# Neighbourhood attention: bias tiles loaded ready-made by DMA, gate spreads ahead of value products, first q/k pair loaded during the GLA stage, norm sums behind the first slots' turns

## The reference, cut to what matters

```python
def neighbourhood_attention(q, k, v, k_ctx, v_ctx, rpb, rows):
    # q,k,v [B,H,S,d]; window of 8 rows x 16 columns round each token, plus all context keys
    win_rows = jnp.clip(r_idx - kh // 2, 0, rows - kh)[:, None] + jnp.arange(kh)
    win_cols = jnp.clip(c_idx - NA_KW // 2, 0, GRID_W - NA_KW)[:, None] + jnp.arange(NA_KW)
    dcol = win_cols - c_idx[:, None] + (NA_KW - 1)
    def one_row(r):
        drow = rws - r + (NA_KH - 1)
        bias = rpb[:, drow[None, :, None], dcol[:, None, :]]
        s_loc = einsum(qr, kw) * scale + bias
        s_ctx = einsum(qr, k_ctx) * scale
        p = softmax(concatenate([s_loc, s_ctx]))
        return p_loc @ vw + p_ctx @ v_ctx

def combine(o, na, z):           # o: GLA output, na: NA output, z: gate input
    g = head_rmsnorm(merge_heads(o), gla_norm, GLA_HEADS)
    return (concatenate([g, merge_heads(na)]) * silu(z)) @ w_out
```

## Time and profile before

| | us |
|---|---|
| median of 3 runs | 3959.82 (3958.52 to 3967.68) |
| the profiled execution, whole | 3962.81 |
| its span | 3959.9 |
| PE busy in the span | 3876.0 (98%) |
| DVE / ACT / POOL busy | 1831.3 / 973.5 / 935.2 |
| mean granted clock, share of full | 0.991 |

### The profile page before, as it was taken

One profiled execution on the slowest core, in us unless ns is written; L12 is line 12 of the kernel. 1 busy time (PEld: TensorE's weight loads), 2 busy tenths in 40 slices (PEclk: granted clock), 3 DMA queues, 4 the chain that ended last, 5 costly groups with the idle time before them and its releaser, 6 DMA issues. The chain is left out here.

```text
span 3959.9 us, 48043 instructions
## 1 busy us (share of the span) xinstructions
PE 3876.0 (98%) x18138; PEld 2409.1 (61%) x18138; DVE 1831.3 (46%) x3905; ACT 973.5 (25%) x1837; POOL 935.2 (24%) x992
## 2 busy tenths in 40 slices
PE   8999999999999999999999999999999999999998
PEld 4688997786558568567544565656544444444447
DVE  3227884676243366556476222222556442313134
ACT  4224332333124311155225211111122000000000
POOL 0005774001111111134132112113132122222223
PEclk9999999999999999999999999999999999999999
DMA  5420003111211122141131112123243211111113
GB/s 196 152 90 11 8 9 68 42 48 54 85 67 39 51 67 65 59 150 40 48 109 55 53 41 67 45 71 106 81 146 127 75 33 47 48 43 43 43 48 101
DMA packets 113715, 270.22 MB, mean 68 GB/s; under 512 B 15623, under 2 KB 45177, under 8 KB 112398
## 3 DMA queue, kind: packets, MB, share of 16 engines
q1 hardware_dynamic: 106512, 251.81, 19.3%
q0 software_dynamic: 5920, 13.25, 1.4%
q10 hardware_dynamic: 1056, 2.10, 0.2%
HBM read 218.53 MB, written 50.87 MB: 68 GB/s over the span
## 5 line engine op out<-in xcount | busy, mean ns | idle before, releaser
L452 PE MATMUL upper_banks<-sbuf 128*128 128x512 f32 (+1 forms) x2016 | 771.4, 545 | 1.5 <-issue 1.1
L3358 PE MATMUL upper_banks<-sbuf 128*128 128x512 f32 x1400 | 617.1, 596 | 5.0 <-ACT sbuf L3635 3.5
L452 PEld LDWEIGHTS upper_banks<-sbuf 128*128 128x128 f32 x2016 | 382.4, 190 | 388.7 <-issue 374.7
L3358 PEld LDWEIGHTS upper_banks<-sbuf 128*128 128x128 f32 x1400 | 263.3, 191 | 317.9 <-issue 308.2
L2502 PE MATMUL gla_prod<-sbuf 128*128 128x512 f32 x560 | 247.6, 593 | 0.3 <-DVE sbuf L2534 0.3
L608 DVE TENSOR_TENSOR sbuf<-upper_banks,sbuf 128x512 f32<-128x512 f32 (+1 forms) x140 | 81.9, 585 | 283.2 <-PE upper_banks L452 282.6
L404 POOL TENSOR_TENSOR sbuf<-sbuf 128x512 f32<-128x512 f32 x36 | 47.4, 1316 | 655.0 <-DMA sbuf<-in_w_mlp_out 306.9
L1039 PE MATMUL mla_banks<-sbuf 128*128 128x128 f32 x1344 | 175.9, 278 | 5.6 <-POOL sbuf L878 4.4
L2502 PEld LDWEIGHTS gla_prod<-sbuf 128*128 128x128 f32 x560 | 103.6, 190 | 119.9 <-issue 117.4
L1662 PE MATMUL mls_banks<-sbuf 128*128 128x512 f32 x392 | 175.1, 593 | 0.3 <-DVE sbuf L2079 0.3
L1039 PEld LDWEIGHTS mla_banks<-sbuf 128*128 128x128 f32 x1344 | 162.9, 192 | 10.5 <-POOL sbuf L878 7.3
(11 more groups left out here) (564 smaller groups left out, 6599.1 us busy)
## 6 DMA issues: line engine op xcount, KB each, us to landing
sbuf<-in_l_w_in SPq DMA_DIRECT2D x59, 512.0 KB, 4.0
sbuf<-in_w_in SPq DMA_DIRECT2D x52, 512.0 KB, 4.5
sbuf<-in_w_mlp_out SPq DMA_DIRECT2D x40, 512.0 KB, 3.6
sbuf<-in_w_mlp_in SPq DMA_DIRECT2D x32, 512.0 KB, 3.7
sbuf<-in_l_w_mod SPq DMA_DIRECT2D x24, 512.0 KB, 6.2
scratch_gates<-sbuf SPq DMA_DIRECT2D x48, 256.0 KB, 2.0
sbuf<-in_l_w_mod SPq DMA_DIRECT2D x8, 1024.0 KB, 16.6
sbuf<-in_l_w_out SPq DMA_DIRECT2D x16, 512.0 KB, 3.7
```

The lines of the kernel that those rows point to most:

```text
L452: last = nc.tensor.matmul(bank_of(n, c)[:, 0:wd], lw[:, k * P:(k + 1) * P], right_operand(c, base, tw, k, o, wd, to), start=k == 0 and c i ...
L3358: last = nc.tensor.matmul(pb, lw[:, k * P:(k + 1) * P], rhs, start=k == 0 and c in ("P1", "P2", "P5"), stop=k == 3, skip_group_check=True)
```

## The change

- **Bias by DMA.** A new input `na_bias` of 64 x 8192 holds every 64 x 64 bias tile ready. SP loads each half of each `mids` and `edge` tile (64 partitions, 2 KB each) directly, 4 transfers a tile, 20 tiles. One-hot matrices, `table_part`, `table_evict` and POOL's copies go. The factor 8 of the table goes too: q is scaled by 1/8 in the GLA stage instead, in the evictions that exist already.
- **First pair during GLA.** q and k of pair 0 are loaded by SP in the GLA stage after the first z store, to where `na_block` expects them; buffers of the GLA stage move for it. Scores of slot 0 wait for that transfer only. v has its own semaphore.
- **Norm sums.** `gla_sums(0)` and `(1)` follow the scores of slot 0, `(2)` and `(3)` follow the first turns of slots 0 and 1. The four products into the unread bank go. DVE copies the sums to SBUF (32 columns), since their bank is used by slot 1.
- **ACT.** Only `zn[0]` gets its Silu ahead of the slots. The Silu of four `zg` tiles stands after `soft(2)`, that of `zn[1]` to `zn[3]` and the root after `soft(5)`.
- **Spreads ahead.** In slots 8 to 23 the two spreads of the norm factors stand before the value products.
- `zg` lies in `U`, where the table was, so pair 1 no longer waits for POOL's gates.

The diff, cut to its core:

```diff
@@ gla_layer, SP
+                if n == first_z:
+                    for e in range(NE):
+                        sp.wait_ge(stored[e], ...)
+                    sp.dma_start(first_keys[:, 0:NLAT], nq_dram[0:P, :]).then_inc(first_in, 16)
+                    sp.dma_start(first_keys[:, NLAT:], nk_dram[0:P, :]).then_inc(first_in, 16)
@@ na_block, SP
-            for r in range(2):
-                sp.dma_start(lhs[64 * r:64 * r + 33, :], io["rpb"]).then_inc(hot_in, 16)
-                sp.dma_start(hot[r], io["rpb_hot"][:, 4096 * r:4096 * (r + 1)]).then_inc(hot_in, 16)
+            def load_bias(dst, h, e, rr, landed):
+                s0, r0 = NA_FIRST[e]
+                a, d0 = na_rows(s0, r0 + rr)
+                o = NCTX + 64 * a
+                sp.dma_start(dst[64 * rr:64 * rr + 64, o:o + 512], io["na_bias"][:, (16 * h + d0) * 64:(16 * h + d0 + 8) * 64]).then_inc(landed, 16)
+            sp.dma_start(zn[:, 0, :], z_dram[4 * P:5 * P, NCTX:T]).then_inc(zn_first, 16)
+            sp.wait_ge(cleared, 1)
+            middle(0)
+            border(0)
+            load_values(0)
+            border(1)
+            sp.wait_ge(cleared, 2)
+            middle(1)
             sp.dma_start(gl[:], io["l1_gla_norm"]).then_inc(gl_in, 16)
-            load_pair(0)
             for j in range(4):
+                sp.dma_start(zg[j], z_dram[j * P:(j + 1) * P, NCTX:T]).then_inc(zg_in, 16)
+            for j in range(1, 4):
                 sp.dma_start(zn[:, j, :], z_dram[(4 + j) * P:(5 + j) * P, NCTX:T]).then_inc(zn_in, 16)
+            load_keys(1)
+            load_values(1)
...
+            for e in range(2, len(edges)):
+                p = 2 + (e - 6) // 4
+                lead = e in (6, 10)
+                if lead:
+                    middle(p)
+                border(e)
+                if lead:
+                    sp.wait_ge(pv, NU * (p - 1))
+                    load_keys(p)
+                    load_values(p)
+                    if p == 2:
+                        sp.dma_start(H[:, :, NCTX:T], h_dram...).then_inc(h_back, 16)
@@ na_block, PE
-            gla_sums(0)
-            gla_sums(1)
-            for x in range(4):
-                nc.tensor.matmul(banks[:, 5, :], ident[:], osum[:, x, 0:512], start=True, stop=True)
-            pe.wait_ge(hot_in, 64)
-            for b in range(8):
-                table_part(b)
             for i in range(-2, NS + 1):
                 if i + 2 < NS:
                     scores(i + 2)
+                if i == -2:
+                    gla_sums(0)
+                    gla_sums(1)
                 if 0 <= i < NS:
                     turn(i, range(2, nb[i]))
-                if i == -2:
-                    gla_sums(2)
-                    gla_sums(3)
                 if i >= 1:
                     weigh(i - 1)
                 if 0 <= i + 1 < NS:
                     turn(i + 1, range(2))
+                if i in (-1, 0):
+                    gla_sums(3 + i)
@@ na_block, ACT
+            act.wait_ge(zn_first, 16)
+            nc.scalar.activation(zn[:, 0, :], zn[:, 0, :], ACT.Silu).then_inc(zn_up, 1)
             soft(0)
             for i in range(NS):
                 copy(i)
                 if i + 1 < NS:
                     soft(i + 1)
+                if i == 1:
+                    act.wait_ge(zg_in, 64)
+                    for j in range(4):
+                        last = nc.scalar.activation(zg[j], zg[j], ACT.Silu)
+                    last.then_inc(zsil, 1)
+                if i == 4:
+                    act.wait_ge(zn_in, 48)
+                    for j in range(1, 4):
+                        last = nc.scalar.activation(zn[:, j, :], zn[:, j, :], ACT.Silu)
+                    last.then_inc(zn_up, 1)
+                    act.wait_ge(gcopied, 1)
+                    nc.scalar.activation(gcol[:], gcol[:], ACT.Sqrt, bias=eps, scale=1.0 / P).then_inc(grooted, 1)
@@ na_block, DVE
-            for b in range(8):
-                table_evict(b)
+            dve.wait_ge(cleared, 3)
...
+                if i == 0:
+                    dve.wait_ge(osum1, 4)
+                    nc.vector.tensor_copy(gcol[:], banks[:, 7, 256:288]).then_inc(gcopied, 1)
```

249 lines of the change are left out of this document (97 added, 152 removed).

## The result

| | before | after |
|---|---|---|
| median, us | 3960.83 (3958.52 to 3967.68, 4 runs) | 3938.65 (3936.03 to 3940.51, 4 runs) |
| the profiled execution, whole / span | 3962.81 / 3959.9 | 3938.22 / 3936.0 |
| mean granted clock, share of full | 0.991 | 0.992 |

The ratio of the two is 0.994, with a 95% interval of 0.9928 to 0.9952. The changed kernel is 22.2 us faster; the forecast was 15.8 (3959.82 to 3944). The direction and the place were right, and the size was 6.4 us short. The lower end of the stated range, 3938.5, stood for 21.3 us gained on 3959.82; the measured gain is beyond that. Measured once more later (changed_again), the same pair of kernels is 16.3 us apart, with the same gain inside the NA stage.

The account below looks back on a forecast made before the run. PE, busy in 98% of the span, was taken to bound the kernel. 19.4 us gained by slot 3, less 3.7 for ACT's insertions, the rest 0, gave 15.7: from 3959.82 to 3944 us, range 3938.5 to 3952.5.

Parts of the forecast that it names:

- The low start: Start of NA: PE enters about 1677.2 at clock 0.50; scores of slot 0 take 3.35 us, sums 0 and 1 6.51.
- The choice of 1703: Start of the scores of slot 3, taken between 1700.7 and 1705.0; 19.4 us gained against 1722.4.
- the forecast's early case: Head of NA: clock rises during scores of slot 1; scores of slot 3 at 1699.7, about 1700.7 with DVE's work.
- The first tile: First bias tile lands at 1682.6 to 1684.6, `biased` at 1685.5 to 1687.5; PE waits 0 to 0.5 us.
- ACT's insertions: Silus and root behind soft(2) and soft(5) cost PE 1.35 and 2.4 us, together 3.7, range 2.5 to 5.
- Later bias tiles are issued two border slots ahead: SP's queue: tiles issued about 20 us ahead arrive in time despite 4 MB of h between; cost 0.
- Spreads at nothing: Slots 8 to 23: spreads ahead of value products mean same products and same waits, so 0 us.
- 1: Clock stays low through the first slots; two low slots cost 8 us, 7.7 gained, 3952 us; chance 0.17.
- 2: ACT's insertions not covered: 13.5 us lost, 3954 us, or 3951 with the page's drain; chance 0.10 for both.
- 3: Narrow bias transfers are slow, ACT waits for `zg`; at 50 GB/s 27.5 us lost, 3972 us; chance 0.04.
- 5: Another wait holds the first slots where the table did; 0 to 3 us gained, 3958 us; chance 0.05.
- 4: Early clock rise and full cover: slot 3 at 1700.7, 2 us lost to ACT, 3940 us; chance 0.14.

Follow-up runs that it names:

- changed_again: The changed kernel itself, unedited, measured again with the third set of runs; 3944.65 us, ratio 0.9941 to 0.9967 against the kernel before.
- late_start: Changed kernel, but PE's first scores also wait for ACT's first square; 3938.83 us.
- sums_first: Changed kernel with all four norm sums directly behind the scores of slot 0, none behind the turns; 3937.67 us.
- spreads_back: Changed kernel with the norm spreads of slots 8 to 23 behind the value products again; 3940.82 us.
- border_first: Changed kernel with the third border tile's transfers issued ahead of pair 1, the gains and the memory input; 3941.02 us.
- tile_late: head_and_act with the third border tile back behind pair 1, the gains and the memory input; 3940.91 us, one run.
- head_and_act: Changed kernel with third border tile early, first bias tile issued first without waiting for POOL, and ACT's second insertion cut in three; 3940.61 us.
- spreads_only: Kernel before, with only the norm spreads of slots 8 to 23 moved ahead of the value products; 3960.31 us, ratio 0.9986 to 1.0005.
- act_spread: border_first with ACT's second insertion cut in three, behind soft(4), soft(6) and soft(7); 3933.57 us, ratio 0.9912 to 0.9941.

## Why the prediction was right or wrong

- **What bounds the kernel**: right. The gain is on PE's own path, in the head, and the stage behind moved with it (out to the end 2063.32 for 2062.57).
- **The low start**: wrong, 1.1 of the 5.4 us by which the head was missed. "I expect the same low start" took the clock from the earlier trace rows, where PE had paused for 3.27 us, although the step itself put PE's start 2.2 us behind the last GLA product. The pause was 1.85, and the stage started at full clock. late_start puts a pause of 3.30 back, and the clock falls at once. But slot 1 waits for the first tile anyway, so only 12.1 for 11.0 us at that mark were lost to this step.
- **The choice of 1703**: the step that failed most, 4.3 of the 5.4 us. From the scores of slot 1 to those of slot 3 the forecast had 15.9 us (1687.1 to 1703), and it took 11.60. The clock was back at the end of the scores of slot 1, as in the forecast's early case, which gives 1700.7 and so 2.3 us. That case itself was 2.0 us too long: the transposes put at 1.8 took 0.97 (1687.57 to 1688.54), and the 1.0 us added for DVE did not show. Against the early rise stood that the clock falls behind sums with one column. It did so for sums 0 and 1 (and for all in sums_first), not for sums 2 and 3 between turns and scores, which ran in 1.84 us each. With the rise as late as in spreads_back this stretch takes 16.0 us, the forecast's value: which of the two comes is a matter of the execution, and no step of the forecast or run here says why.
- **The first tile**: its time was right, PE's was not. It was put at 1682.6 to 1684.6 and landed at 1682.0, which is 1683.3 in the time of before; the scores of slot 1 start at 1684.7 (1686.0 in that time), inside the 1685.5 to 1687.5 for `biased`. But PE, put at 1687.1 with its slow work, was done 3.71 us before the scores could start, where 0 to 0.5 had been expected. Faster work in front was given back to the transfer. The forecast's own test, no wait of DVE for a tile over 1 us, failed with 7.22 us; it did not follow from its numbers, which had the scores of slot 0 end at 1680.6 and the tile land 2 us later at the least.
- **ACT's insertions**: the first 0.28 us in place of 1.35, the second 2.13 in place of 2.4, both by border_first. Their sum, 2.4 in place of 3.7, is just under the 2.5 to 5 that was given. The longest wait for ACT there was 1.38. Round the first insertion PE waits 0.24, 0.16 and 0.26 us for ACT, and the 0.70 us that it would have waited for DVE in that slot takes up most of it, as the step had allowed for.
- **4.1 us lost from slot 3 to 9 is right by accident.** The forecast's 3.7 was ACT's. Measured, 1.7 came on top from the border tile with the slow scores behind it, though it hid part of ACT's second insertion (36.00 without the stop, 33.87 without both, 38.50 with the stop alone).
- **"Later bias tiles are issued two border slots ahead ... still within that"**: wrong for the third border tile. The step reckoned with the 4 MB of h and not with what stands ahead of this tile in SP's queue, an issue of 6.60 us and 1 MB of `mem`. tile_late against head_and_act prices its place at 4.6 us where ACT doesn't cover it.
- **Spreads at nothing**: wrong by 2.6 us. "Same products, the same waits" counted instructions, and the order of the groups changes how closely they follow each other: 2.93 for 3.28 us for the same 40 records. spreads_only and spreads_back show it from both sides, in the profile; the medians of spreads_only can't tell it from nothing.
- **POOL, the scaling of q, the loads in the GLA stage at nothing**: nothing seen against it. L1039's first row to GLA end takes 1380.6 us before and 1380.8 after, with all of the GLA stage in it.
- **Rivals.** 1 didn't hold: the scores of slots 2 and 3 take 1.78 and 1.56. It was nearer than that shows, since in spreads_back's execution they took 3.36 and 2.64. 2 didn't: 2.4 us, not 13.5. The Trainium skill (ScalarE: Activation LUTs, What ACT_TABLE_LOAD costs) puts 1.38 us of drain on every switch. The trace doesn't agree: the Silus end at 1720.66 and the load of the root starts at 1720.67, the next operation follows 1.30 us after it, and act_spread, with three loads more than the change, is 2.1 us shorter from slot 3 to 9 than border_first. No run shows the drain. 3 did not hold: eight narrow transfers were issued in 4.96 us, and ACT's Silu of `zg` starts at 1698.98 without a wait, though one narrow tile came late elsewhere. 5 did not hold. 4, at 3940, came nearest, for part of its reason: the mark was earlier still (1696.3, or 1697.6 in the time of before), and the cover not full.

In sum, 15.7 forecast and 23.9 in the span: 5.4 more in the head (1.1 the low start, 2.3 the choice against the early rise, 2.0 the early case itself), 2.6 from the spreads, -0.4 from slot 3 to 9, and 0.6 from what no edit touches.

## What to carry to other kernels

Take the duration of work after a change from rows with the clock that the change will leave there: look at how long PE pauses ahead of it in the new order, not at the rows of the old. For each transfer that a slot needs, read everything that is queued ahead of it, small ones too, and give it a place by its due time. A heavy insertion on an engine with 2.7 us of slack a slot can be all but free when it is cut up, even if that costs more table loads: pieces of 2.9 to 4.6 us, their loads counted, cost nothing that shows here, where 7.1 us in one piece cost 2.13. And take a mark ahead of the point where executions part: slot 1 tells 2 us apart here, slot 3 doesn't.

## What the runs showed of the hardware

- PE's pause decided the clock behind it: with a pause of 1.84 to 1.86 us scores of slot 0 took 1.78 us in all ten profiles that have it, with 3.30 us 2.86, with 7.53 us 3.36 (one profile each).
- Products with one column did not hold the clock although PE counted as busy: it fell to 0.65 and 0.50 during 64 records of them in a row, fell within 32 in changed_again (4.60 us for 3.73), and stayed at 1.00 where each 16 records stood between 128x512 products.
- The same 40 records in another order took 10% less: 2.93 us with the gate spreads between transposes and value products, 3.28 with them behind the value products. Why is open; weight loads of 64 and of 128 columns follow each other in another order, which no run took apart.
- When the clock comes back after such a pause is not the same in each execution of one program: by 1688 and after 1690 in two executions of the changed kernel, 1.2 us at slot 3, and only by 1699 in spreads_back, 4.4 us at slot 3.
- The issue of a transfer of 4 KB (`final_norm`) took 6.60 us on SP's queue, beside two others of 4 KB at 0.43 us.
